# The scan's x turned on VectorE and through DRAM instead of TensorE, and a reordered entry, in a one-core model of two transformer layers

## The reference

```python
h = _rmsnorm(x, norm_pre[i, 0])
zxbcdt = h @ ssd_w_in              # z, x, B, C (8 groups of 128 states) and dt (64 heads of 64)
# x, B, C: causal convolution with 4 taps, then SiLU; dt: softplus
# per group of 8 heads: y = scan(x * dt, decay exp(cumsum(dt * A)), B, C) + d_skip * x
# y = rmsnorm(y * silu(z)) @ ssd_w_out
```

## Time and profile before

| | us |
|---|---|
| median of 3 runs | 2646.73 (2645.4 to 2646.84) |
| the profiled execution, its own time | 2646.47 |
| its span, first to last instruction | 2644.8 |
| PE busy | 2627.6 (99%) |
| DVE busy | 1800.3 (68%) |
| ACT busy | 1325.3 (50%) |
| POOL busy | 243.9 (9%) |

### The profile page before, as it was taken

The page is one execution under the profiler, slowest core; times in us unless marked ns, Lnnn a source line. Parts: engine busy times, 40 slices in busy tenths (PEclk is TensorE's granted clock), DMA queues, the critical chain, the costliest instruction groups (busy, mean ns, idle before and its releaser), DMA issues.

```text
span 2644.8 us, 38671 instructions
## 1 busy us (share of the span) xinstructions
PE 2627.6 (99%) x14178; PEld 2245.1 (85%) x14178; DVE 1800.3 (68%) x2273; ACT 1325.3 (50%) x1655; POOL 243.9 (9%) x289
## 2 busy tenths in 40 slices
PE   9999999999999999999999999999999999999998
PEld 8888888888888888888888888888888888888887
DVE  6988888855767676767644576765566767676444
ACT  6555554544766555554544464444465454544443
POOL 2433333300000000000000010210000000000000
PEclk9999999999999999999999999999999999999999
DMA  8666666575455555555555475455555555555552
GB/s 248 197 196 217 210 203 213 196 265 194 144 178 188 191 188 192 184 191 185 211 196 191 165 238 183 149 172 202 180 176 190 190 190 190 190 190 208 192 196 103
DMA packets 257451, 508.13 MB, mean 192 GB/s; under 512 B 17190, under 2 KB 113674, under 8 KB 237152
## 3 DMA queue, kind: packets, MB, share of 16 engines
q1 hardware_dynamic: 248880, 476.81, 53.7%
q0 software_dynamic: 8256, 29.75, 3.2%
q10 hardware_dynamic: 240, 0.56, 0.1%
HBM read 499.12 MB, written 4.28 MB: 190 GB/s over the span
## 4 chain that ended last, share of the span: by engine, by line
PE 96%; DVE 2%; ACT 1%; issue 1%; DMA 0%; POOL 0%; SPq 0%; POOLq 0%; ACTq 0%; DVEq 0%
PE PB L1396 14%; PE T L1396 14%; PE T L1755 12%; PE PB L1755 11%; PE PB L1589 10%; PE T L1758 6%; PE PB L1758 6%; PE PB L1592 5%; PE PB L1341 4%; PE PB L1343 4%; PE PB L1342 4%; PE T L1627 1%; PE T L1688 1%; DVE hT L2022 1%; DVE w_lo L1993 0%
## 5 line engine op out<-in xcount | busy, mean ns | idle before, releaser
L1993 DVE TENSOR_TENSOR w_lo<-raw,w_hi 128x2048 fp32r<-128x2048 f32 (+3 forms) x468 | 1046.6, 2243 | 554.2 <-ACT w_hi L839 552.4
L839 ACT ACTIVATE w_hi<-raw 128x2048 fp32r<-128x2048 f32 (+3 forms) x468 | 868.8, 1858 | 872.1 <-PE T L1396 383.7
L1755 PE MATMUL T<-hT,w_hi 128*128 128x512 f32 x1408 | 489.7, 391 | 0.0
L1755 PE MATMUL PB<-hT,w_hi 128*128 128x512 f32 x1280 | 444.6, 391 | 0.0
L1758 PE MATMUL T<-hT,w_lo 128*128 128x256 f32 x1408 | 394.3, 280 | 0.0
L1589 PE MATMUL PB<-hT,w_hi 128*128 128x512 f32 x1184 | 376.1, 399 | 0.0
L1758 PE MATMUL PB<-hT,w_lo 128*128 128x256 f32 x1280 | 358.4, 280 | 0.0
L1755 PEld LDWEIGHTS T<-hT,w_hi 128*128 128x128 f32 x1408 | 263.4, 187 | 58.0
L1396 PE MATMUL PB<-w_hi,hT 128*128 128x512 f32 x1120 | 304.6, 390 | 1.5 <-DVE w_lo L1993 1.5
L1396 PE MATMUL T<-w_hi,hT 128*128 128x512 f32 x1120 | 302.6, 391 | 0.0
L1755 PEld LDWEIGHTS PB<-hT,w_hi 128*128 128x128 f32 x1280 | 239.4, 187 | 52.5
(11 more groups left out here) (324 smaller groups left out, 2547.1 us busy)
## 6 DMA issues: line engine op xcount, KB each, us to landing
raw<-in_ffn_w_up_dram SPq DMA_DIRECT2D x88, 1024.0 KB, 5.0
raw<-in_w_up_dram SPq DMA_DIRECT2D x88, 1024.0 KB, 5.1
raw<-in_ssd_w_in_dram SPq DMA_DIRECT2D x64, 1024.0 KB, 5.4
raw<-in_ffn_w_down_dram SPq DMA_DIRECT2D x44, 1024.0 KB, 4.8
raw<-in_w_down_dram SPq DMA_DIRECT2D x44, 1024.0 KB, 4.8
raw<-in_w_in_dram SPq DMA_DIRECT2D x40, 1024.0 KB, 5.1
raw<-in_ssd_w_out_dram SPq DMA_DIRECT2D x32, 1024.0 KB, 4.9
raw<-in_ssd_w_in_dram SPq DMA_DIRECT2D x64, 256.0 KB, 3.8
```

Of the source, the lines that this page charges most:

```text
L839: nc.scalar.activation(dst, src, ACT.Copy).then_inc(hi_ready, 1)
L1755: ins = nc.tensor.matmul(banks[f][:, :], wh[:, c, s], both, start=(k == 0), stop=False)
L1993: V.tensor_tensor(dst, src, h.bitcast(F32), ALU.subtract).then_inc(lo_ready, 1)
```

## The change

- **x turned without PE.** For groups 0 to 6 `back_xs` is gone. VectorE turns `xc` in four operations of blocks of 32x32 (`turn_x`, after the split of the next B/C unit's second quad); POOL stores the result to DRAM with two transfers and loads it back with eight, in the order that puts tokens on the partitions, into `yt` (`move_x`). `xs_back` then reads it from SBUF, in sixteen operations of 128 columns and one of 512, and stands after `bc_out` instead of after the split of the second wide quad. The last group keeps the old way.
- **The scan** is hooked in after the second wide quad instead of the first, and waits for `xdt_ready`.
- **The entry.** The first x tile is loaded ahead of the first weights, and each quarter's x ahead of its weights. The weights are copied, differenced and waited for chunk by chunk (four parts a quarter). PE's warming products are 6 and 7 instead of 4, 6 and 4, and the transposes of the second tile of x move into the first products.

```diff
@@ SP
-            for j in range(4):
-                load_bcd(j)
-                for tt in range(TT):
-                    at = slice(j * BLK, (j + 1) * BLK)
-                    sp.dma_start(xt[:, tt, at], I["x"][0, tt * P:(tt + 1) * P, at]).then_inc(x_landed[j], 16)
+            load_x(0, 0, x0_landed[0])
+            load_bcd(0)
+            load_x(0, 1, x0_landed[1])
+            for j in range(1, 4):
+                for tt in range(TT):
+                    load_x(j, tt, x_landed[j])
+                load_bcd(j)
@@ POOL
+            def move_x(g):
+                pool.wait_ge(x_turned, g + 1)
+                nc.gpsimd.tensor_tensor(vb[:, 1001:1002], half[:, 0:1], half[:, 1:2], ALU.add)
+                for tt in range(TT):
+                    pool.dma_start(xs_d[:, tt * BLK:(tt + 1) * BLK], u[:, tt * BLK:(tt + 1) * BLK]).then_inc(x_stored[tt], 16)
+                for tt in range(TT):
+                    pool.wait_ge(x_stored[tt], g * 16 + 16)
+                    nc.gpsimd.tensor_tensor(vb[:, 1002 + tt:1003 + tt], half[:, 0:1], half[:, 1:2], ALU.add)
+                    for a in range(4):
+                        pool.dma_start(yt[32 * a:32 * (a + 1), tt * BLK:(tt + 1) * BLK].rearrange("j (b e) -> j b e", b=4),
+                                       bass.AP(xs_d.tensor, tt * BLK + a * P, [[4 * L, 32], [32 * 4 * L, 4], [1, P]]))\
+                            .then_inc(x_moved[tt], 16)
...
             exponents(0)
-            with nc.gpsimd.Fori(0, GROUPS - 1) as i:
-                pool.wait_ge(tf[3], i + (TB["ssd"][3] + 1))
-                nc.gpsimd.tensor_tensor(idle[:, 0:1], half[:, 0:1], half[:, 1:2], ALU.add)
-                exponents(i + 1)
+            move_x(0)
+            with nc.gpsimd.Fori(0, GROUPS - 2) as i:
+                next_exponents(i)
                 move_y(i)
+                move_x(i + 1)
+            next_exponents(GROUPS - 2)
+            move_y(GROUPS - 2)
@@ ACT
+                act.wait_ge(raw_landed[j], landed(U_SSD))
+                for c in range(4):
+                    nc.scalar.activation(quad(w_hi, j, BCD)[:, c], quad(raw, j, BCD)[:, c], ACT.Copy).then_inc(hi_ready if c == 3 else part_hi, 1)
...
                 if prev:
                     hi(q + 8, land(2), 0)
+                    for tt in range(TT):
+                        act.wait_ge(x_stored[tt], g * 16)
                     half_low(q + 6, 1, u_xs[:, 0:2, :])
@@ PE
             def diagonal(g):
                 pe.wait_ge(m_ready, g + 1)
-                pe.wait_ge(te[1], t1_back(g) + 1)
+                pe.wait_ge(xdt_ready, g + 1)
...
-                    half_unit(q, range(4), lambda j: (quad(w_hi, j, 2 * NST), quad(w_lo, j, 2 * NST)), 0, {1: late(back_xs)})
+                    half_unit(q, range(4), lambda j: (quad(w_hi, j, 2 * NST), quad(w_lo, j, 2 * NST)), 0, {})
...
-                half_unit(q + 4, (0, 1), both_wide, 1, {0: late(scan)} if prev else {0: turn_other_rows})
+                half_unit(q + 4, (0, 1), both_wide, 1, {1: late(scan)} if prev else {0: turn_other_rows})
@@ VectorE
+            def turn_x(g):
+                dve.wait_ge(xc_ready, g + 1)
+                for k in range(4):
+                    ins = V.transpose(xct[:, k], xc[:, k, :].rearrange("p (t i) -> p t i", i=32))
+                ins.then_inc(x_turned, 1)
...
             def xs_back(g):
+                def scaled(dst, tt, factor):
+                    for r in range(2):
+                        for s in range(2):
+                            ins = V.tensor_tensor(in_heads(dst[:, tt, :], r, s), x_rows[:, tt, r, s], by_pair(factor, g, r), ALU.mult)
+                    return ins
                 for tt in range(TT):
+                    dve.wait_ge(x_moved[tt], g * 64 + 64)
+                    ins = scaled(xdt, tt, dt[:, tt, :])
+                    if tt == 0:
+                        own(ins)
+                        V.tensor_tensor(heads(bd), heads(xdt[:, 0, :]), by_head(dte, g), ALU.mult).then_inc(bd_ready, 1)
+                ins.then_inc(xdt_ready, 1)
+                for tt in range(TT):
+                    ins = scaled(yg, tt, d_skip)
+                ins.then_inc(yg_made, 1)
...
                 for j in range(4):
                     lo(q + 4, j)
-                    if j == 1 and prev:
-                        xs_back(g - 1)
...
                 if prev:
                     bc_out(g)
+                    xs_back(g - 1)
                 lo(q + 8, 0)
...
                 lo_next(1)
+                if nxt:
+                    turn_x(g)
                 lo_next(2)
```

More of the change, by code:

```diff
@@ L369, in program @@
         x_landed = [sem(f"x_landed{b}") for b in range(NB)]
+        x0_landed = [sem(f"x0_landed{tt}") for tt in range(TT)]
+        part_hi, part_lo = sem("part_hi"), sem("part_lo")
         mem_landed = [sem(f"mem_landed{tt}") for tt in range(TT)]
@@ L382, in program @@
         bd_ready, yg_ready = sem("bd_ready"), sem("yg_ready")
+        x_turned, x_stored, x_moved, xdt_ready = sem("x_turned"), [sem(f"x_stored{a}") for a in range(TT)], [sem(f"x_moved{a}") for a in range(TT)], sem("xdt_ready")
+        yg_made = sem("yg_made")
         y_turned, y_moved, yt_free = sem("y_turned"), sem("y_moved"), sem("yt_free")
@@ L1376, in up @@
                         split(1, j)
-                    if not by_tile:
+                    if not by_tile and not entry:
                         pe.wait_ge(lo_ready, q + j + 1)
@@ L1498, in norm_transposes, with turn_group @@
                     ins.then_inc(full, 1)
-            def turn_group(n, b):
-                for tt in range(TT):
+            def turn_group(n, b, tiles=range(TT)):
+                for tt in tiles:
                     bank, full, empty, uses = h_bank(n, tt, b)
-                    if n == N_X:
+                    if n == N_X and b == 0:
+                        pe.wait_ge(x0_landed[tt], 16)
+                    elif n == N_X:
                         pe.wait_ge(x_landed[b], 32)
@@ L1629, in diagonal, with scan @@
                     ins.then_inc(tf[2 + c], 1)
-            def scan(g):
-                off_diagonal(g)
+            def scan(g, last=False):
+                off_diagonal(g, last)
                 diagonal(g)
@@ L1670, in _ @@
             z_out = lambda: pe.wait_ge(proj_evac, E_Z + GROUPS - 1)
-            down("wout", [(0, (0, 1), lambda: pe.wait_ge(xs_joined[1], GROUPS), {1: lambda: back_xs(last)}),
-                          (0, (2,), z_out, {3: lambda: scan(last)}),
+            down("wout", [(0, (0, 1), lambda: pe.wait_ge(xs_joined[1], GROUPS), {1: back_last_xs}),
+                          (0, (2,), z_out, {3: lambda: scan(last, True)}),
                           (1, (0,), tile_one(0), {}),
@@ L2157, in _, with lo_bcd @@
             signal(cols_ready)
-            for j in range(4):
-                lo_unit(U_SSD, BCD, (j,))
+            def lo_bcd(j):
+                for c in range(4):
+                    if c < 3:
+                        dve.wait_ge(part_hi, 3 * j + c + 1)
+                    else:
+                        dve.wait_ge(hi_ready, 4 * U_SSD + j + 1)
+                    V.tensor_tensor(quad(w_lo, j, BCD)[:, c], quad(raw, j, BCD)[:, c], quad(w_hi, j, BCD)[:, c].bitcast(F32), ALU.subtract)\
+                        .then_inc(lo_ready if c == 3 else part_lo, 1)
+            h_lo(N_X, 0, "norm_pre", 0, (0,))
+            lo_bcd(0)
+            h_lo(N_X, 1, "norm_pre", 0, (0,))
+            for j in range(1, 4):
                 for tt in range(TT):
                     h_lo(N_X, tt, "norm_pre", 0, (j,))
+                lo_bcd(j)
             def other_cols():
@@ L2355, in _ @@
             group(GROUPS - 1, True, False)
-            xs_back(GROUPS - 1)
+            last_xs_back()
             decayed(GROUPS - 1)
-            gather(GROUPS - 1)
+            gather(GROUPS - 1, True)
             squared(GROUPS - 1)
```

92 lines of the change are left out of this document (57 added, 35 removed).

## The result

| | before | after |
|---|---|---|
| median, runs side by side | 2646.27 (2645.4 to 2646.84) | 2668.45 (2666.07 to 2671.59) |
| ratio | | 1.0084, 95% interval 1.0072 to 1.0097 |
| span of the profiled execution | 2644.8 | 2666.1 |

The change makes the kernel slower by 22 us. The prediction had the sign, but forecast 8.7 us, and its range ended at 2664.

The account below looks back on a forecast made before the run. PE, busy 99% of the span, was taken to bound the kernel. 2646.5 - 6.1 (transposes) - 2.7 (entry) + 17.5 (waits at `cb_products`) = 2655.2 us, range 2637 to 2664.

Parts of the forecast that it names:

- Part 1: Groups 0 to 6: the transposes of x leave PE, 0.87 us each, 6.1 us gained.
- Part 2: x turned on VectorE and sent through DRAM by POOL: cost 0, covered by about 5 us.
- Part 3: Scan a quad later: PE waits 2.5 us at `cb_products` in groups 1 to 7, 17.5 us lost.
- Part 4: Entry: first product at 8.5, 3.8 us earlier; gain between 1.5 and 3.8 us, taken as 2.7.
- A: Rival: wait at `cb_products` absent or below 0.5 us, 2638 to 2641; chance 0.22, shared with a no-entry-gain rival.
- B: Rival: wait at `cb_products` between 0.5 and 2.0 us, 2641 to 2652 us; chance 0.18.
- C: Rival: x comes back late from DRAM, delaying `gather`; 2669 us with 2 us late; chance 0.06.
- D: Rival: shared port lock for the whole instruction, waits of 6 us in seven groups, 2680 us; chance 0.02.

Follow-up runs that it names:

- without POOL's collision: The scan part with POOL's three operations on the exponents cut to an eighth of their columns: 2639.2 us, ratio 0.9973.
- one-pass kernel: The scan part with POOL's exponents made by sixteen operations that subtract and clamp at once, same values: 2682.96 us, ratio 1.0145.
- scan part: The changed kernel with the entry of before, so x turned without PE and the scan a quad later: 2661.7 us, ratio 1.0058.
- first exponents light: The scan part with POOL's exponents of group 0 alone cut to an eighth of their columns: 2656.86 us, ratio 1.0038.
- mended entry: Kernel before with the changed entry, weights split ahead of h, transposes after a quarter's first product, quarter 1's before the wait for tile 1: 2646.87 us, ratio 1.0005.
- POOL's order turned: The scan part with POOL issuing the exponents' load and y's transfers before computing on the exponents: 2644.85 us, ratio 0.9995.

## Why the prediction was right or wrong

**Part 1** (6.1 us for PE's transposes) was right: without POOL's collision a group is 0.88 us shorter.

**Part 2** (the round trip costs nothing) was right in the changed kernel. x is turned at 273.31, back in time for `xs_back` at 290.98 without a wait, and its operations take 0.21 to 0.22 each instead of 0.27. Only in group 1 is `bd` late, by 1.15 us. That the cover is POOL's free queue, as the text said, is shown by the one-pass kernel, where that queue was full.

**Part 3**: the mechanism was right in each step, POOL's operations on top of the second split and the taps, SiLU late, PE waiting at `cb_products`, seven times. The loss was 5.7 where 6.1 was taken. The wait in the usual group was mis-sized, 1.8 for 2.5. From the end of the scan (about 238.3, where `gather`'s second addition starts) to the end of the taps it took 17.8 us instead of 18.4: 0.4 less lost beside POOL, 0.2 less in the clean operations, and PE came after 16.8 us, as reckoned (due at 256.98 - 1.88 = 255.10). That POOL started 6.2 us after the scan and not 7.7 made little difference, since both of its stages still lay on the split and the taps. The sum of the waits, 14.6, is within 3 us of the 17.5, and that is partly luck: five usual groups were 0.7 too dear each, and group 1, 3.5, was too cheap. The step that failed for group 1 is "it recurs in groups 1 to 7, since each group counts from its own scan". Group 1 also carries what group 0 left, and group 0's collision was in the trace of before.

**What the sum lacked** is the rest of the scan part: 15.9 measured (21.5 - 5.6) against 14.6 + 1.2 - 6.1 = 9.7 from the listed waits. Of the missing 6.2, 1.6 to 1.9 lie in each of the groups 1, 2 and 7, and 0.26 in each of the others (61.12 - 58.98 - 1.88, for one). A usual group has one wait, so the wait seems to cost 0.26 us beyond its row. Group 1 has four waits, two of them for `w_lo`, 0.45 and 0.35 us, and 4 x 0.26 + 0.80 gives 1.84 of its 1.87 (an estimate from these rows). In groups 2 and 7 the half-speed stretch of the clock rows is what stands there, some 1.5 us each. Runs that differ in it agree: in the scan part alone the clock reads 1.00 behind group 6's wait (1.39 us, 434 to 438), and nothing is missing in group 7 (61.74 - 2.49 - 59.25, the last being the 60.12 of before less 0.87); with the first exponents light it reads 1.00 behind group 1's wait (2.00 us, 124 to 132), and only 0.24 is missing in group 2, as in a usual one. The prediction had neither, the cost beyond the wait nor the clock behind it, in its sum. No run changed the clock alone, so the division is read from rows.

**Part 4** failed outright: 5.6 us lost for 2.7 gained. The first product came at 9.49 for 8.5, and at full speed (0.38 us), which would have left 2.8 us, as forecast, though not for the reason given: it came 1.0 later and nothing was lost to the clock. The step that failed is "then the work up to 31.10 follows as before". The diff moved the transposes of the next x from behind a quarter's first product to behind its first half, and I read that hunk only for the first quarter. From the transposes to the next product there are 4.5 us of splitting, and PE had 2.8 us of transposes and products to do in them (27.91 to 30.70). The runs divide it: transposes late 2.7, weights behind h 1.9, both together with the earlier transposes of quarter 1 5.1. And the mended entry shows a second fault of that step: the first wide quad lands no earlier, so the gain of the first product didn't get past 31 us there.

**The balance.** From the forecast 8.7 us to the 21.5 measured: the entry 8.3 more (5.6 lost for 2.7 gained), the waits at `cb_products` 2.9 less, the scan's wait in group 1 1.2 more, and 6.2 more that the sum didn't have. With the entry as forecast the kernel would have come out near 2660, without the last term near 2662, both inside the range: it took the two together to leave it.

**The rivals.** A's condition (VectorE loses under 3.5 us) and B's wait (0.5 to 2.0) stood on the same term; the usual groups were B's, 1.8, and the rest of the kernel was worse than either. C was reached only in the one-pass kernel. D, the lock for the whole instruction, would have needed waits of 6 us (7 by the prediction's own row, with 10.8 lost in place of 6.1) and is out. The range was too narrow because every case in it had the entry between 1.5 and 3.8 us of gain or at nothing: none had it as a loss, although the text elsewhere bounds unknown costs from both sides.

## What to carry to other kernels

Work taken off the engine that bounds the kernel pays only if what it feeds keeps its place in time; here moving the scan by 5.6 us put VectorE's six taps under POOL's long operations, and what brought the time back to that of before was to move POOL's operations, not VectorE's. When a collision can't be shrunk, place it where the engine that suffers has idle time afterwards, which the windows and waits of the trace show. And in an entry, count from each step that starts a chain (here a transpose) to the product that needs it, for every round and not only the first.

## What the runs showed of the hardware

- VectorE's operations with two inputs in SBUF are held up beside POOL's long ones: 7.71 us for 2.91 (taps), 5.18 for 1.23, 4.01 for 0.68 (a square pass of 512 columns). Transposes of 32x32 blocks are not: two took 1.30 us at 291.42 in the kernel before, beside POOL's long operation (291.62 to 296.99), and 1.30 at 292.11 in the kernel with POOL's order turned, where POOL computes nothing. The Trainium skill, SBUF — State Buffer (section SBUF: two separate sides), states just such a block, for VectorE with two SBUF inputs against a GpSimd operation that reads SBUF, for the whole instruction. The runs agree on which of these operations, not on how long: beside POOL's operation of 5.4 us (309.45 to 314.82) a split that began 0.4 us after its start took 4.30 for 1.21 and ended 0.6 us ahead of it. The largest loss, 3.95 us, was beside the two of 1024 columns, 3.77 us together.
- POOL pays as well: its two operations of 1024 columns took 3.77 us where VectorE had one long operation beside them, and 5.80 beside a split and taps. No run took the two apart.
- POOL's operation with a column as its scalar, 128x128, took 1.26 us, and beside sixteen of them in a row VectorE's taps took 3.14 for 2.91: nearly no block, though it reads SBUF too. The reason was not looked into.
- The granted clock fell to about 0.6 for some us after waits of PE of 3.50 us, of 2.60 in the entry (at 18.94) and, at 440.01, of only 1.80; after one of 1.80 at 195.86 it stayed at 1.00, and so it did after one of 2.00 in the kernel with the first exponents light.
